# A two-block network on one core: 12 of 16 gate chunks issued inside the attention, and S5's four units fed together

## The reference

```python
u = _rmsnorm(h, norm_mix[i])
(nq, kc, vc, ksl, vsl, kwn, vwn, ng, sq, sk, sv, ga, gb) = jnp.split(u @ w_in[i], pts, axis=-1)
o_a = _nsa(nq, kc, vc, ksl, vsl, kwn, vwn, ng, ...)         # compressed + selected + window attention, 8 heads
o_b = _banded_attention(sq, sk, sv, SWA_WINDOW, swa_sinks)   # window 128, 8 heads, sinks
merged = jax.nn.sigmoid(ga) * (o_a @ w_branch_a) + jax.nn.sigmoid(gb) * (o_b @ w_branch_b)
h = h + merged @ w_out
```

```python
bu = einsum('bsgh,gph->bsgp', u, bb)                 # feed the states (complex)
x_t = a * x_(t-1) + bu_t                              # scan over time (complex)
y = gelu(Re(einsum('bsgp,ghp->bsgh', x, c)) + d_skip * u)
y = y * sigmoid(y @ w_glu + b_glu)
```

## Time and profile before

| what | us |
|---|---|
| median of 3 runs (2992.05 to 3009.61) | 2995.52 |
| the profiled execution | 2989.28 |
| its span, first to last instruction | 2987.5 |
| PE busy in the span | 2740.0 (92%) |
| DVE busy | 1947.1 (65%) |
| POOL busy | 1283.5 (43%) |
| ACT busy | 1037.2 (35%) |

### The profile page before, as it was taken

One profiled execution on the slowest core, in us unless ns is written; L12 is line 12 of the kernel. 1 busy time (PEld: TensorE's weight loads), 2 busy tenths in 40 slices (PEclk: granted clock), 3 DMA queues, 4 the chain that ended last, 5 costly groups with the idle time before them and its releaser, 6 DMA issues. The chain is left out here.

```text
span 2987.5 us, 38641 instructions
## 1 busy us (share of the span) xinstructions
PE 2740.0 (92%) x14085; PEld 2295.0 (77%) x14085; DVE 1947.1 (65%) x3130; ACT 1037.2 (35%) x1635; POOL 1283.5 (43%) x607
## 2 busy tenths in 40 slices
PE   7998999778989998979988999998999969999996
PEld 5887877336778887758876789998999958888785
DVE  5444232683454444366555267778999969999998
ACT  4232321453233223222022233334655524444342
POOL 3443442002434443423042356773222247777773
PEclk9999999699999999989798999999999989999998
DMA  5443341002234443322002245557999999999993
GB/s 177 136 152 116 106 151 50 1 1 64 91 99 141 150 131 113 99 84 78 15 1 64 83 133 158 165 171 282 344 341 353 343 306 373 376 370 376 377 374 137
DMA packets 186680, 528.83 MB, mean 177 GB/s; under 512 B 14032, under 2 KB 96336, under 8 KB 166480
## 3 DMA queue, kind: packets, MB, share of 16 engines
q1 hardware_dynamic: 80208, 292.66, 30.4%
q0 software_dynamic: 18432, 134.23, 11.5%
q10 hardware_dynamic: 87936, 100.68, 9.8%
HBM read 475.08 MB, written 52.43 MB: 177 GB/s over the span
## 5 line engine op out<-in xcount | busy, mean ns | idle before, releaser
L344 POOL TENSOR_TENSOR ring_low<-ring,ring_high 128x1024 fp32r<-128x1024 f32 x323 | 795.0, 2464 | 1164.4 <-ACT ring_high L311 1164.4
L395 PE MATMUL ps<-u_high,ring_high 128*128 128x512 f32 (+1 forms) x1824 | 695.9, 382 | 44.5 <-DVE u_low L618 17.4
L396 PE MATMUL ps<-u_low,ring_high 128*128 128x512 f32 (+1 forms) x1824 | 686.9, 377 | 0.0
L397 PE MATMUL ps<-u_high,ring_low 128*128 128x512 f32 (+1 forms) x1824 | 686.3, 376 | 0.0
L311 ACT ACTIVATE ring_high<-ring 128x1024 fp32r<-128x1024 f32 x355 | 374.5, 1055 | 618.4 <-PE ps L397 549.4
L395 PEld LDWEIGHTS ps<-u_high,ring_high 128*128 128x128 f32 x1824 | 345.6, 189 | 111.3 <-issue 40.9
L396 PEld LDWEIGHTS ps<-u_low,ring_high 128*128 128x128 f32 x1824 | 346.1, 190 | 52.5 <-issue 2.0
L397 PEld LDWEIGHTS ps<-u_high,ring_low 128*128 128x128 f32 x1824 | 345.7, 190 | 52.6
L2346 POOL DMA_INDIRECT fetched_rows<-in_peer_uv,fetch_index x128 | 165.1, 1290 | 339.7 <-DVE ps L2366 302.4
L344 POOL TENSOR_TENSOR ring_low_more<-ring,ring_high_more 128x1024 fp32r<-128x1024 f32 x96 | 243.2, 2546 | 32.3 <-ACT ring_high_more L311 31.7
L2901 DVE TENSOR_TENSOR expert_coef_low<-expert_product,expert_coef_high 128x384 fp32r<-128x384 f32 x128 | 214.7, 1677 | 0.1
(11 more groups left out here) (427 smaller groups left out, 4863.4 us busy)
## 6 DMA issues: line engine op xcount, KB each, us to landing
ring<-in_peer_u SPq DMA_DIRECT2D x128, 512.0 KB
ring<-in_peer_uv SPq DMA_DIRECT2D x128, 512.0 KB
ring<-in_ffn_gu SPq DMA_DIRECT2D x88, 512.0 KB
ada_weights<-in_ada_w SPq DMA_DIRECT2D x48, 512.0 KB, 3.8
ring<-in_ffn_down SPq DMA_DIRECT2D x48, 512.0 KB
expert_acts<-kept_acts ACTq DMA_DIRECT2D x128, 192.0 KB, 4.0
expert_weights<-weight_stage ACTq DMA_DIRECT2D x24, 1024.0 KB, 8.9
group_acts<-expert_acts ACTq DMA_DIRECT2D x16, 1536.0 KB
```

The source lines that it names most:

```text
L344: pool.tensor_tensor(k.lows[p], k.ring[:, s], k.highs[p].bitcast(F32), ALU.subtract)\
L395: pe.matmul(out, k.highs[p][:, w], high, start=first, stop=False)
L396: pe.matmul(out, k.highs[p][:, w], low, start=False, stop=False)
L397: last = pe.matmul(out, k.lows[p][:, w], high, start=False, stop=final)
```

## The change

Three things move. (1) `GatesBeside` issues gate chunks 0 to 11 inside the attention block: PE does a quarter of a chunk (6 matmuls) in each unit, between `score(n+2)` and `turn(n)`, into bank 7; every fourth unit ACT copies the bank to `k.pair` (`rope_pair`), SP stores it to a DRAM tensor `gate_logits`, and ACT splits the next chunk, whose low part POOL makes. All three kinds of `mix` now use bank 6. (2) `gate_tiles` keeps chunks 12 to 15, loads the 12 stored tiles back, and DVE scales and ACT sigmoids them; the rounding of `o_t` goes from DVE to ACT. (3) S5 feeds all four units at once into banks 0 to 7, uses banks 0 to 3 again for lags, `within` and the reading (now unit pairs interleaved), and the Gelu, the gate's product and the recurrence's preparation run in the same block, by tile.

```diff
+    def multiply(self, pe, n):          # GatesBeside; per = 4
+        j, part = n // self.per, n % self.per
+        self.stream.multiply_part(pe, j, KD * part // self.per, KD * (part + 1) // self.per)
+    def take(self, act, n):
+        if n % self.per or n == 0:
+            return
+        k, j = self.k, n // self.per - 1
+        self.stream.wait_products(act, 0, j)
+        if j >= 2:
+            act.wait_ge(self.stored[j % 2].sem, 16 * (j // 2))
+        act.activation(self.kept[:, j % 2], k.ps[:, self.BANK], ACT.Copy).then_inc(k.emptied[self.BANK].sem, 1)
+        if j + 2 < BESIDE:
+            self.stream.split_high(act, 0, j + 2)
...
                 for n in range(len(units)):                     # attend, PE
                     if n + 2 < len(units):
                         score(n + 2)
+                    gates.multiply(pe, n)
                     turn(n)
...
                 for n in range(len(units)):                     # attend, ACT
+                    gates.take(act, n)
                     if n + 1 < len(units):
                         exp(n + 1)
                     copy(n)
...
+            @block.sync
+            def _(sp):
+                gates.load(sp)
+            @block.gpsimd
+            def _(pool):
+                gates.stream.split_low(pool)
...
+                beside.wait_stored(sp)                          # gate_tiles, SP
+                for b in range(3):
+                    sp.dma_start(dst[:, 4 * b:4 * (b + 1)], k.dram["gate_logits"][4 * b:4 * (b + 1)]...)
+                    if j == 0:                                  # gate_tiles, ACT
+                        for n in range(KD):
+                            act.activation(split.high[:, n], source[:, n], ACT.Copy).then_inc(rounded.sem, 1)
+                    else:
+                        for n in range(4 * (j - 1), 4 * j):
+                            act.wait_ge(rescaled.sem, n + 1)
+                            act.activation(dst[:, n], dst[:, n], ACT.Sigmoid)
...
-                for a in range(4):                              # s5_chunks, PE
-                    for at in range(SPAN):
-                        for c in range(2):
-                            feed(0, a, at, c)
-                            mm = feed(1, a, at, c)
-                mm.then_inc(fed.sem, 2)
-                lags()
-                within()
-                for r in range(2):
-                    pe.wait_ge(state.sem, r + 1)
-                    feed_unit(r + 2)
-                    read_unit(r)
-                read_unit(2)
-                read_unit(3)
+                for a in range(4):
+                    for at in range(SPAN):
+                        for c in range(2):
+                            for r in range(UNITS):
+                                mm = feed(r, a, at, c)
+                mm.then_inc(fed.sem, 1)
+                pe.wait_ge(state.sem, 1)
+                lags()
+                pe.wait_ge(placed.sem, UNITS)
+                for a in range(4):
+                    if a == 2:
+                        pe.wait_ge(state.sem, 2)
+                    within(a)
+                for a in range(4):
+                    mm = read_states((0, 1), a)
+                mm.then_inc(read.sem, 1)
+                pe.wait_ge(state.sem, 4)
+                for a in range(4):
+                    read_states((2, 3), a).then_inc(done.sem, 1)
+                pe.wait_ge(s.glu_loaded.sem, 16)
+                for a in range(4):
+                    pe.wait_ge(acted.sem, a + 1)
+                    for m in range(4):
+                        mm = pe.matmul(k.ps[:, 4 + m], s.glu_w[:, a, m * P:(m + 1) * P], u[:, a], start=a == 0, stop=a == 3)
```

More of the change, by code:

```diff
@@ L46 @@
 PROJ = 16
+BESIDE = 12
 VEC = {}
@@ L400, in multiply_once, with multiply_part @@
                 after(j)
+    def multiply_part(self, pe, j, lo, hi):
+        k, p = self.k, j % self.parts
+        bank, out, parts, opens, closes, _ = self.chunks[j][1][0]
+        if lo == 0:
+            pe.wait_ge(k.low_ready[p].sem, k.low_ready[p].at(j // self.parts + 1))
+            pe.wait_ge(k.emptied[bank].sem, k.emptied[bank].at(j))
+        for m in range(lo, hi):
+            tile, high, low = parts[m]
+            w = slice(tile * P, (tile + 1) * P)
+            pe.matmul(out, k.highs[p][:, w], high, start=m == 0, stop=False)
+            pe.matmul(out, k.highs[p][:, w], low, start=False, stop=False)
+            last = pe.matmul(out, k.lows[p][:, w], high, start=False, stop=m == len(parts) - 1)
+        if hi == len(parts):
+            last.then_inc(k.used[p].sem, 1)
     def wait_products(self, eng, i, j):
@@ L890, in copy_tiles, with gate_tiles @@
         shifted.finish()
-def gate_tiles(k, weights, tiles, dst, moving, source, split):
-    stream = plain_stream(k, weights, tiles, 4, KD, moving)
+def gate_tiles(k, weights, dst, moving, beside, source, split):
+    stream = plain_stream(k, weights, SLOTS, SLOTS, KD, moving)
     rounded = k.tiles_rounded
@@ L1312, in attend @@
         mixed = sem("att_mixed")
-        emptied = [sem(f"att_emptied{b}") for b in range(2)]
+        emptied = sem("att_emptied")
+        gates = GatesBeside(k, ctx, len(units))
         def blocks_of(n):
@@ L1350, in mix @@
                     first, count = blocks_of(4 * group)
-                    bank, which = (7, 1) if kind == 2 else (6, 0)
                     for g in range(2):
                         pe.wait_ge(copied[g].sem, 4 * group + 4)
-                    if kind != 1 and qt >= 1:
-                        pe.wait_ge(emptied[which].sem, qt)
-                    out = [k.ps[HD * g:HD * (g + 1), bank] for g in range(2)]
+                    if kind == 2 or (kind == 0 and qt >= 1):
+                        pe.wait_ge(emptied.sem, 2 * qt + kind // 2)
+                    out = [k.ps[HD * g:HD * (g + 1), 6] for g in range(2)]
                     if kind == 0:
@@ L1422, in _ @@
                         empty(n // 4 - 1)
+                gates.take(act, len(units))
                 empty(len(units) // 4 - 1)
+            @block.sync
[4 more added lines that the diff above has]
+                gates.stream.split_low(pool)
             @block.vector
@@ L1482, in _ @@
                     copy(n)
+    gates.stream.finish()
+    return gates
 def branches(k, weights, gates, o, merged):
@@ L2074, in turns_of_chunks, with s5_chunks @@
                 twice()
[L2077 removed]
+def s5_chunks(k, s, u, x, recurrence):
     nc = k.nc
+    rounded = k.tiles_rounded
+    part = k.after
+    w = (k.total, k.rs)
+    out = x[:].rearrange("p b c t -> p (b c) t")
     with ExitStack() as tmp:
[L2084 to L2094 removed]
+        sem = lambda name: Signal(tmp, nc, name)
+        fed, state = sem("s5_chunks_fed"), sem("s5_states_ready")
+        lagged, cleared, placed = sem("s5_lags_multiplied"), sem("s5_lags_cleared"), sem("s5_lags_placed")
+        read, done, skipped = sem("s5_states_read"), sem("s5_tiles_multiplied"), sem("s5_skip_added")
+        acted, gated, product, mixed = (sem("glu_" + n) for n in ("gelu_ready", "gate_ready", "product_ready", "mixed"))
         chunks = lambda ap: ap.rearrange("p (c s) -> p c s", s=SPAN)
```

199 lines of the change are left out of this document (96 added, 103 removed).

## The result

The changed kernel takes 2910.81 us (median of 4 runs, 2909.42 to 2916.12) against 2993.78 for the kernel before beside it: ratio 0.9721, 95% interval 0.9687 to 0.9755. The profiled execution took 2909.72 us (span 2908.0) against 2989.28 (2987.5), 79.6 us less, and all but 1.5 of it lies in three stretches. The kernels' times are medians of executions in the faster of the program's two states; one later execution of the changed kernel, 3129.76 us, fell in the slower one and is left out.

A forecast was written before the change was run, and what follows sets the result against it. TensorE was taken to bound the gate stage, DVE to pace the attention, PE and DVE to alternate in S5. -66.8 + 20 - 22 = -69 from 2989.28 gives 2920; the median stands 6 above, so 2925 us, range 2902 to 2955.

The forecast's parts named there:

- the likeliest case: Whole kernel: the forecast's main case, total from 2912 to 2938 us, chance 0.50.
- Gate stage, -66.8: Gate stage: 12 chunks move out, 25.8 us remain of 92.6, so the stage gives back 66.8 us.
- PE's sum in the attention, 159 us: Attention: PE's own work over 48 units, with the added products and the mixes, sums to 159 us.
- DVE's sum, 122 + 16 + 12 x 2.2 = 164: Attention: DVE's 122 us of work, 16 waiting behind mixes, and 2.2 for each of twelve POOL splits.
- larger of the two in each group: Attention: the larger of PE's and DVE's time in each of 12 groups gives 169 us, 176 with start and tail.
- The sign that I named: Attention: DVE operations of L1462's kind would show lengths near 2 us about twelve times.
- Ends, 7 us: Attention: a start of 1 us and a tail of 6 behind the last unit, barrier included.
- S5, -22: S5: feeding four units at once and closing the gate's tiles in the same block ends it at 1503.5, not 1525.8.
- the port bites fully: Attention rival: every split holds DVE its whole length, late exponentials add 1 us; +36 to +45, total about 2945; chance 0.15.
- four row groups don't overlap: S5 rival: feed 15 us longer, reading 7 longer, total about 2947 at most; chance 0.15.
- the clock might fall in the attention: Attention rival: PE at 1.2 GHz throughout, attention +155 us, total near 3060; chance 0.03.
- Hides altogether: Attention rival: splits fall in DVE's idle time, attention costs +7 us, total about 2912; chance 0.13.

The follow-up runs named there:

- the run with two products: Changed kernel with one of the three products left out for the chunks beside the attention; 2899.49 us.
- the runs with hardly any products: Changed kernel with a single matmul for each chunk beside the attention: 2926.24 us with full POOL splits, 2903.14 us with splits cut to 8 columns.
- the second profile: The changed kernel, unaltered, profiled once more; S5 took 91.0 us instead of 93.3.
- the single matmuls: Changed kernel with one matmul of the 24 of each chunk beside the attention, full splits kept; 2926.24 us, ratio 0.9770.
- one product of three: Changed kernel with only the high-by-high product of each chunk beside the attention, loads, splits and copies kept; 2913.27 us, ratio 0.9727.
- the attention's half alone: Changed kernel with S5's two blocks put back as they were before; 2958.32 us, ratio 0.9881.

## Why the prediction was right, and where its terms were off

2925 was forecast, 2910.81 measured, inside the range and 1 us under the low end of the likeliest case; the parts of the sum that were off by more than 1 us all erred on the dear side. On the profiled execution the sum was 10.8 us too dear (-68.8 for -79.6), 6.7 of it in the attention and 3.4 in S5.

- **Gate stage, -66.8.** Measured -66.0. PE waited 2.23 us for POOL's split of the third chunk, where 1.8 was forecast; behind the stored tiles' loads, 3 x 1024 KB landing in 8.0 us, PE waits for nothing.
- **PE's sum in the attention, 159 us.** Near, 4 us too low: 163.4 busy, 96.5% of the stage, clock 1.00 as forecast. The stage is this sum and its ends; the run with two products shows that the last 96 products cost 12.4 us, 129 ns each, while the first 192, with the splits and copies and with the clock's rise to 1.00, cost 0.9.
- **DVE's sum, 122 + 16 + 12 x 2.2 = 164.** This is the step that failed. It was 136.3 busy and 14.5 waiting, 151. The splits stretched DVE by 13 us, 1.1 each and not 2.2, on two-element operations; its waits behind the mixes fell to 14.5. So DVE was not the one that PE waited for, the "larger of the two in each group" (169) should have been PE's sum, and removing the splits gains 1.3 us at the same clock. The price itself was near for a stage where DVE is on the chain: 2.0 us each by the runs with hardly any products, with what the clock took in it. The sign that I named, twelve operations of L1462's kind near 2 us, came only in those runs.
- **Ends, 7 us.** 163.4 to 169.3: 5.9. Right.
- **From the profiled execution to the median.** I added 5 us, since the median of before stood 6 above its profiled execution; for the changed kernel the two are 1.1 apart. The other four of the 14 us between 2925 and 2910.81 are this.
- **S5, -22.** The feed (14.77 of 15), the lags' start, `within` (12.72 of 12.8) and the first reading (7.13 of 7.3) came as written. Too dear was the close: I let ACT change its function after the product for 1.3 us, and the first sigmoid came without that wait. With the product (14.0, not 14.5) that is 1.8 of the 3.4 us; the rest is tenths, the second reading's end 0.9 early among them. The reading's 7.3 hit by luck: it is 0.114 halved, the 0.114 had some 4 us at 0.50 in it, and at 1.00 the old rate of 0.103 became 0.056, by a little less than half. The stage took 91.0 in the second profile, so the size of this miss, 3.4 or 5.7, depends on the clock of the execution.
- **Rivals.** That the port bites fully is refuted for this kernel; with the single matmuls, one edit away, they cost 2.0 us each, near their own 2.4. That four row groups don't overlap is refuted by the feed. That the clock might fall in the attention did not happen: it stood at 1.00 with 288 and with 192 products, at 0.88 with 96 and at 0.76 with 12. "Hides altogether", 2912, gave the nearest time, and its mechanism was nearly right, since the splits cost 1.3 us of the stage; but its +7 was +13.3, for PE's sum came out higher. That its total still came within 2 us is luck: S5 and the step to the median were off the other way.

## What to carry to other kernels

Before pricing a stall, ask which engine's own sum sets the stage after the change: here eleven splits beside a busy TensorE cost 1.3 us, and in the same code with hardly any matmul work 22. And look at the clock before you count removed matmuls as a gain: with one product of three the stage was 12.9 us longer than with two, at a lower clock and with the splits stretching DVE more, and ten matmuls that nobody reads, put in two pauses, were worth 20 us. When halves of a change don't add up, look for the clock in stages that neither half touches.

## What the runs showed of the hardware

- TensorE stood at 1.2 GHz (0.50) for 40 us while never idle, in hgrn's scores of the attention's half alone: 387 ns a matmul instead of 275, 16.5 us lost. They were back in the run with the two pauses ahead, 6.6 and 3.2 us, filled; the kernel before has these pauses and no such fall in its profile.
- Records of S5's feed overlap fourfold over row groups: 64, 128 and 256 of them take 14.86, 14.90 and 14.77 us. The Trainium skill (TensorE: Matmul & The Clock Gate, LDWEIGHTS) gives 107 ns for a load of 128 columns; by an estimate from that figure, 256 loads one after another would take 27 us. The trace differs: its loads last 181 to 205 ns each, and a record comes every 58 ns, so the loads do not run one after another here.
- In the reading, whose matmuls fill 32 output partitions each, alternating between two such groups gives 56 ns a record at clock 1.00, changing after every 16 records 88 and after every 64 records 103.
- Beside POOL's two-input splits of 1024 columns, DVE's operations of two elements with both inputs in SBUF (L1558, 161 to 408 ns in the mean) and its tensor_scalar of 128 to 512 columns (to 2579 ns) are stretched. Its reductions and copies out of PSUM (758 and 452 ns) and its reciprocals (157 ns) keep their lengths.
